# Hybrid encoder block on one core: the query product of the memory attention as seven block products, with weight sums kept in device memory and the key turn moved into the memory projection

## What is computed

```python
h = rms_norm(x, norm_xa_pre[l])
mn = rms_norm(mem, norm_mem[l])
q = (h @ xa_wq[l]).reshape(B, S, XA_HEADS, XA_HEAD_DIM)          # 1024x1024 by 1024x1024
kv = (mn @ xa_wkv[l]).reshape(B, M, 2, XA_HEADS, XA_HEAD_DIM)    # 256x1024 by 1024x2048
s = jnp.einsum('bshd,bmhd->bhsm', q, kv[:, :, 0]).astype(jnp.float32) * (XA_HEAD_DIM ** -0.5)
```

## Time and profile before

| | us |
|---|---|
| median of 3 runs | 1470.1 |
| range of the runs | 1470.03 to 1470.73 |
| profiled execution | 1470.84 |
| its span in the profile | 1468.9 |
| PE busy | 1431.9 |
| POOL busy | 785.4 |
| DVE busy | 681.4 |
| ACT busy | 588.4 |

### The profile page before, as it was taken

How to read it: one execution, slowest core, us unless ns; L and a number is a source line. 1 busy time by engine, 2 the same in 40 slices (tenths; PEclk the granted TensorE clock), 3 DMA queues, 4 the chain that set the end, 5 groups by cost and what they waited for, 6 DMA issues and landing times.

```text
span 1468.9 us, 20008 instructions
## 1 busy us (share of the span) xinstructions
PE 1431.9 (97%) x7192; PEld 1197.3 (82%) x7192; DVE 681.4 (46%) x1125; ACT 588.4 (40%) x1225; POOL 785.4 (53%) x607
## 2 busy tenths in 40 slices
PE   7999999998999999999999999999999999999998
PEld 7999999756988777877778888888888888767886
DVE  5181048586884760006136843333333323243868
ACT  6111112676633661125346533333333333434454
POOL 1454445001963365420235577777777775599753
PEclk9999999999999999999999999999999999999999
DMA  4311112000024143110124333333333224933364
GB/s 190 96 50 45 48 47 63 0 2 1 23 85 181 55 147 108 50 43 1 58 65 165 122 101 103 99 108 108 108 108 96 90 87 151 365 102 93 100 204 155
DMA packets 106292, 140.33 MB, mean 96 GB/s; under 512 B 8160, under 2 KB 61664, under 8 KB 106208
## 3 DMA queue, kind: packets, MB, share of 16 engines
q1 hardware_dynamic: 102480, 129.00, 27.0%
q10 hardware_dynamic: 3728, 10.24, 1.9%
HBM read 110.64 MB, written 28.57 MB: 95 GB/s over the span
## 4 chain that ended last, share of the span: by engine, by line
PE 84%; DVE 5%; POOL 3%; ACT 3%; DMA 2%; issue 2%; POOLq 0%; SPq 0%; DVEq 0%; ACTq 0%
PE ps L926 24%; PE ps L928 24%; PE ps L927 24%; PE ps L922 4%; PE ps L1273 2%; PE ps L1248 2%; DVE z L2331 1%; PE ps L1053 1%; PE ps L1147 1%; POOL w_lo L801 1%; POOL wd L895 1%; PE ps L1081 1%; DMA gain_b<-f_rows 1%; PE ps L1125 1%; DMA raw<-in_xa_wkv_dram 1%
## 5 line engine op out<-in xcount | busy, mean ns | idle before, releaser
L926 PE MATMUL ps<-w_hi,t_hi 128*128 128x352 f32 (+1 forms) x768 | 268.3, 349 | 3.0 <-DVE t_lo L2451 1.4
L928 PE MATMUL ps<-w_hi,t_lo 128*128 128x352 f32 (+1 forms) x768 | 266.5, 347 | 0.0
L927 PE MATMUL ps<-w_lo,t_hi 128*128 128x352 f32 (+1 forms) x768 | 266.1, 346 | 0.0
L726 POOL TENSOR_TENSOR w_hi<-raw,zero 128x352 fp32r<-128x352 f32 (+1 forms) x84 | 75.2, 895 | 174.5 <-PE ps L928 174.5
L926 PEld LDWEIGHTS ps<-w_hi,t_hi 128*128 128x128 f32 x768 | 145.2, 189 | 15.0 <-DVE t_lo L2451 2.2
L928 PEld LDWEIGHTS ps<-w_hi,t_lo 128*128 128x128 f32 x768 | 145.1, 189 | 10.8
L927 PEld LDWEIGHTS ps<-w_lo,t_hi 128*128 128x128 f32 x768 | 145.2, 189 | 10.4
L815 POOL TENSOR_TENSOR w_lo<-raw,w_hi 128x512 fp32r<-128x512 f32 x32 | 41.7, 1317 | 118.7 <-ACT w_hi L1774 118.7
L730 POOL TENSOR_TENSOR w_lo<-raw,w_hi 128x352 fp32r<-128x352 f32 (+1 forms) x84 | 95.8, 1140 | 6.6
L1542 ACT ACTIVATE z<-ps 128x352 f32 x48 | 22.4, 466 | 162.0 <-PE ps L928 161.5
L2564 DVE TENSOR_TENSOR ev<-ps,ev 128x512 f32<-128x512 f32 x21 | 14.5, 691 | 144.2 <-PE ps L928 144.2
...
## 6 DMA issues: line engine op xcount, KB each, us to landing
...
```

The lines of the kernel that those rows point to most:

```text
L726: nc.gpsimd.tensor_tensor(hi[:, s, 0:width], raw[:, s, 0:width], zero[:, 0:1].broadcast_to([P, width]), ALU.add).then_inc(w_rounded, 1)
L926: nc.tensor.matmul(out, a_hi, b_hi, start=start, stop=False, skip_group_check=onto)
L927: nc.tensor.matmul(out, a_hi, b_lo, start=False, stop=False, skip_group_check=onto)
L928: return nc.tensor.matmul(out, a_lo, b_hi, start=False, stop=stop, skip_group_check=onto)
```

## The change

The two operands are cut in 2x2 blocks: weights A (features of q by input features), tokens B (input features by halves of the tokens). Seven products of 512x512 blocks, in the order 11, 12, S1, S4, S2, S3, 22, take the place of eight; each is four units of four tiles, 12 matmuls a unit, 28 units. 11 and 12 use the weights and tokens as they are (of the first half of the tokens), S1 to S4 use sums of weight blocks, and S1, S4, S2, S3, 22 use or follow sums of token blocks.

- Weight sums: in the input projection SP loads the four blocks of `xa_wq` in four rounds into free columns of `z` (4 transfers of 256 KB a round), GpSimd makes four sums a round, one behind each split of units 12 to 27, SP stores them to `w_sums` in device memory.
- Token sums: the first (b12 - b11) is made on the rows, before they are turned, by a 512-wide subtraction in `pre_rows` for tiles 4 to 7. The others are made from the split parts: `tok_sum` (VectorE, three dependent operations of 128x1024), `tok_round` (ScalarE), `tok_low_part` (VectorE), six times.
- `tq_sum`, `tq_hi`, `tq_lo` lie where x1 was: SP stores x1's eight rows to device memory between the loads of the third memory product, and loads them back behind the query weights, ahead of the output weights.
- Query weights are rounded by ScalarE (`q_round`) and no longer by GpSimd, which keeps the low parts.
- After 11 and 12, ScalarE copies four banks each; after S1, S4, S2, S3 and 22 VectorE adds four banks each to `qX` (`q_join`).
- PE turns the keys between units 4 and 5 of the third memory product, into banks 4 to 7; ScalarE copies them behind its eighth rounding and ahead of the copies of that product. Tiles 4 and 5 are turned into these banks, each half once its bank's key copy is done.
- Loops of SP and GpSimd in the input projection are written out. The semaphores used are old ones at higher counts.

```diff
--- before.py
+++ after.py
@@ -56,14 +56,15 @@
-U_XO = U_Q + 2 * NK
+U_XO = U_Q + 7 * RING
...
-TILES = dict(z=0, oa=56, o=63, kv=77, q=81, xo=95, f=109)
+TILES = dict(z=0, oa=56, o=63, kv=77, q=81, xo=81)
+TURNED_K = TURNED["h2"] + 8
@@ -116,7 +117,17 @@
 def kv_seen(c, t):
-    return ACT_EV["h2"] + 6 * c + t + 1
+    return ACT_EV["h2"] + 6 * c + t + 1 + (4 if c >= 2 else 0)
+def h2_turned(t):
+    return TURNED["h2"] + 2 * t + (4 if t >= 4 else 0)
+PRODUCTS_Q = ("11", "12", "S1", "S4", "S2", "S3", "22")
+WEIGHT_SUMS = ("S1", "S2", "S3", "S4")
...
@@ -441,6 +462,32 @@
     return hi[:, k % RING, 0:ZW], lo[:, k % RING, 0:ZW]
+def sum_stage(r, b):
+    c = (ZP - 1) * ZW if r % 2 == 0 else (ZP - 2) * ZW
+    return z[:, 2 * b:2 * b + 2, c:c + 256]
+def two(ap):
+    return ap.rearrange("p (t f) -> p t f", t=2)
+def q_weights(n):
+    kind, k = PRODUCTS_Q[n // RING], n % RING
+    if kind in WEIGHT_SUMS:
+        return w_sums[WEIGHT_SUMS.index(kind), k]
+    i, j = int(kind[0]) - 1, int(kind[1]) - 1
+    return wq_v[RING * j + k, :, i * 512:(i + 1) * 512]
+def tok_sum_of(i, h):
+    lower, k = slice(0, 512), slice(2 * h, 2 * h + 2)
+    upper, kk = slice(512, 1024), slice(4 + 2 * h, 6 + 2 * h)
+    b11, b12 = (t_hi[:, k, lower], t_lo[:, k, lower]), (t_hi[:, k, upper], t_lo[:, k, upper])
+    b21, b22 = (t_hi[:, kk, lower], t_lo[:, kk, lower]), (t_hi[:, kk, upper], t_lo[:, kk, upper])
+    t2 = (tq_hi[:, k, :], tq_lo[:, k, :])
+    return ((t2, b22, b12), (b11, t2, b11), (b21, b21, t2))[i]
@@ -587,8 +634,31 @@
         sp.dma_start(z[:, t, 0:D], x_v[t]).then_inc(x_in[t], 16)
-    with sp.Fori(1, ZP) as c:
-        piece(c * NK + U_Z, win_v, bass.ds(c * ZW, ZW), ZW)
+    def sums_load(r):
+        if r >= 2:
+            sp.wait_ge(sums_out[r % 2], SUMS_OUT + 64 * (r // 2))
+        for b, (j, i) in enumerate(((0, 0), (1, 0), (0, 1), (1, 1))):
+            sp.dma_start(sum_stage(r, b), two(wq_v[RING * j + r % RING, :, i * 512:(i + 1) * 512])).then_inc(
+                sums_in[r % 2], 16)
+    def sums_store(r):
+        sp.wait_ge(summed_w, SUMMED_W + 4 * (r + 1))
+        for b, n in enumerate((1, 3, 0, 2)):
+            sp.dma_start(two(w_sums[n, r % RING]), sum_stage(r, b)).then_inc(sums_out[r % 2], 16)
+    for n in range(NK, ZP * NK):
+        c, k = divmod(n, NK)
+        load(c * NK + U_Z, k, raw[:, k % RING, 0:ZW], win_v[k, :, c * ZW:(c + 1) * ZW])
+        i = n // RING - 2
+        if n % RING == RING - 1:
+            if n == NK + RING - 1:
+                sp.wait_ge(w_split, NK)
+            if 2 <= i < SUM_ROUNDS + 2:
+                sums_store(i - 2)
+            if i < SUM_ROUNDS:
+                sums_load(i)
@@ -599,8 +669,18 @@
             load(U_KV + c * NK, k, dst, src)
-    with sp.Fori(0, 2) as c:
-        piece(c * NK + U_Q, wq_v, bass.ts(c, 512), 512)
+        if 2 * NK <= n < 3 * NK:
+            t = n - 2 * NK
+            sp.wait_ge(added, t + 1)
+            sp.dma_start(x1_rows[t], x1[:, t, :]).then_inc(x1_out, 16)
+    for i in range(2):
+        sp.wait_ge(sums_out[i], SUMS_OUT + 64 * SUM_ROUNDS // 2)
+    for n in range(7 * RING):
+        load(U_Q, n, raw[:, n % RING, :], q_weights(n))
+    sp.wait_ge(w_used, U_Q + 5 * RING)
+    sp.wait_ge(tok_low, TOK_LOW + 6)
+    for t in range(NT):
+        sp.dma_start(x1[:, t, :], x1_rows[t]).then_inc(x_in[t], 16)
@@ -737,11 +817,31 @@
         nc.gpsimd.tensor_tensor(lo, first_raw(k), hi.bitcast(F32), ALU.subtract).then_inc(w_split, 2 if k else 1)
+    def weight_sums(r, step):
+        a11, a12, a21, a22 = (sum_stage(r, b) for b in range(4))
+        done = SUMMED_W + 4 * r
+        if step == 0:
+            pool.wait_ge(sums_in[r % 2], SUMS_IN + 64 * (r // 2 + 1))
+            nc.gpsimd.tensor_tensor(a21, a21, a22, ALU.add).then_inc(summed_w, 1)
+        elif step == 1:
+            pool.wait_ge(summed_w, done + 1)
+            nc.gpsimd.tensor_tensor(a11, a21, a11, ALU.subtract).then_inc(summed_w, 1)
+        elif step == 2:
+            pool.wait_ge(summed_w, done + 2)
+            nc.gpsimd.tensor_tensor(a12, a12, a11, ALU.subtract).then_inc(summed_w, 1)
+        else:
+            nc.gpsimd.tensor_tensor(a22, a22, a11, ALU.subtract).then_inc(summed_w, 1)
...
+        else:
             split(c * NK + U_Z, U_Z, k, ZW, loads=c * 2)
+        r = n // RING - 3
+        if 0 <= r < SUM_ROUNDS:
+            weight_sums(r, n % RING)
@@ -804,9 +904,11 @@
             mem_low(n)
-    with pool.Fori(0, 2) as c:
-        for k in range(NK):
-            split(c * NK + U_Q, U_Q, k, 512, loads=c * 2)
+    for n in range(7 * RING):
+        k = n % RING
+        pool.wait_ge(q_rounded, Q_ROUNDED + n + 1)
+        nc.gpsimd.tensor_tensor(w_lo[:, k, :], raw[:, k, :], w_hi[:, k, :].bitcast(F32),
+                                ALU.subtract).then_inc(w_split, 1)
...
@@ -1195,11 +1299,26 @@
     def turn_tile(stage, n0, t):
+        def bank_free(half):
+            if t >= 2:
+                pe.wait_ge(dve_ev, DVE_EV[stage] + 2 * (t - 2) + half + 1)
+            if t in (4, 5):
+                pe.wait_ge(act_ev, kv_seen(1, 1) + 4 + 2 * (t - 4) + half + 1)
         turn_rows(t, lambda j: y[:, t, j * P:(j + 1) * P], 4 + 2 * (t % 2),
-                  lambda: pe.wait_ge(scaled, n0 + t + 1),
-                  lambda half: pe.wait_ge(dve_ev, DVE_EV[stage] + 2 * (t - 2) + half + 1) if t >= 2 else None)
+                  lambda: pe.wait_ge(scaled, n0 + t + 1), bank_free)
     pe.wait_ge(dve_ev, DVE_EV["h2"])
+    def turn_keys():
+        pe.wait_ge(act_ev, kv_seen(1, 1))
+        pe.wait_ge(dve_ev, DVE_EV["h2"] + 8)
+        for i in range(4):
+            for j in range(4):
+                kt, mt = divmod(4 * i + j, NM)
+                last = transpose_to(4 + i, j * P, kst[:, mt, kt * P:(kt + 1) * P])
+            last.then_inc(turned, 1)
@@ -1209,35 +1328,52 @@
         product(c * NK + U_KV, NM, 512, lambda t: pe.wait_ge(act_ev, kv_seen(c - 2, t)) if c >= 2 else None,
-                rows_by_weights(m_hi, m_lo, 512), b0=2 * (c % 2), ready=lambda k: kv_ready(c * NK + k))
+                rows_by_weights(m_hi, m_lo, 512), b0=2 * (c % 2), ready=lambda k: kv_ready(c * NK + k),
+                between=turn_keys if c == 2 else lambda: None)
...
         turn_tile("h2", NT + NM, 2 * c + 1)
...
+    def query_product(j):
+        kind = PRODUCTS_Q[j]
+        half, kk = {"11": (0, 0), "12": (0, 4), "S1": (512, 0), "S4": (512, 4), "S3": (0, 0), "22": (0, 4)}.get(kind, (0, 0))
+        high, low = (tq_hi, tq_lo) if kind == "S2" else (t_hi[:, kk:kk + 4, half:half + 512],
+                                                         t_lo[:, kk:kk + 4, half:half + 512])
+        first, b0 = kind in ("11", "S1", "S2"), 4 if kind in ("S1", "S4") else 0
+        for k in range(RING):
+            pe.wait_ge(w_split, U_Q + RING * j + k + 1)
+            if kind in ("S2", "S3", "22") and k % 2 == 0:
+                pe.wait_ge(tok_low, TOK_LOW + 2 * ("S2", "S3", "22").index(kind) + k // 2 + 1)
+            for m in range(4):
+                if k == 0:
+                    if kind == "11":
+                        pe.wait_ge(act_ev, kv_seen(2 + m // 2, m % 2))
+                    elif kind == "12":
+                        pe.wait_ge(q_copied, Q_COPIED + m + 1)
+                    elif kind == "S1" and m == 0:
+                        pe.wait_ge(dve_ev, DVE_EV["h3"])
+                    elif kind == "S4":
+                        pe.wait_ge(q_joined, Q_JOINED + m + 1)
+                    elif kind == "S2":
+                        pe.wait_ge(q_copied, Q_COPIED + 4 + m + 1)
+                    elif kind == "S3":
+                        pe.wait_ge(q_joined, Q_JOINED + 8 + m + 1)
+                    elif kind == "22":
+                        pe.wait_ge(q_joined, Q_JOINED + 12 + m + 1)
+                w = slice(m * P, (m + 1) * P)
+                last = three(ps[:, b0 + m, :], w_hi[:, k, w], w_lo[:, k, w], high[:, k, :], low[:, k, :],
+                             first and k == 0, k == RING - 1, not first)
+                if m == 3:
+                    last.then_inc(w_used, 1)
+                elif k == RING - 1:
+                    last.then_inc(q_done, 1)
+    for j in range(7):
+        query_product(j)
+    pe.wait_ge(q_joined, Q_JOINED + 20)
...
@@ -1733,7 +1863,21 @@
     round_units(RING)
+    def q_round(n):
+        act.wait_ge(w_loaded[n % RING], 16 * ((U_Q + n) // RING))
+        act.wait_ge(w_used, U_Q + n - RING + 1)
+        nc.scalar.activation(w_hi[:, n % RING, :], raw[:, n % RING, :], ACT.Copy).then_inc(q_rounded, 1)
     for c in range(4):
+        if c == 2:
+            for i in range(4):
+                act.wait_ge(turned, TURNED_K + i + 1)
+                nc.scalar.activation(kM[:, 2 * i:2 * i + 2, :], bank(4 + i).rearrange("p (k m) -> p k m", k=2),
+                                     ACT.Copy).then_inc(act_ev, 1)
+        if c == 3:
+            for n in range(3):
+                q_round(n)
@@ -1744,24 +1888,65 @@
```

(90 more changed lines are left out.)

70 lines of the change are left out of this document (35 added, 35 removed).

## The result

The changed kernel takes 1472.88 us (median of 20 runs, 1469.91 to 1476.27) beside 1471.3 us for the kernel before on the same chip (20 runs, 1469.73 to 1472.03). The ratio is 1.0014, 95% interval 1.0008 to 1.0021: slower by 1.6 to 2 us where 1.9 us less was forecast. The direction was wrong; the time is inside the range, close to its upper end.

What follows compares the result with a forecast made beforehand. PE, busy 97% of the span, was taken as the bound. Terms -11.2 + 1.1 + 2.4 + 5.7 + 0.1 = -1.9 us gave 1468.9 against the profiled 1470.84, 1468.2 against the median; range 1462.0 to 1473.0.

Steps and rivals of the forecast that it cites:

- The matmuls: Query product: 336 matmuls, 48 fewer, of the same shape at 0.2336 us each, -11.2 us.
- Weight sums: Input projection: GpSimd's 512-wide sums fit beside its splits within PE's 3.82 us per unit, so 0.
- Stall 1: Query product, unit 17: PE waits for weights rounded behind token sums, 0 to 2.8 us, taken as +2.4.
- Stall 2: Query product, unit 21: the last token sum's chain holds back the weight rounding, 5.1 to 6.0 us, taken as +5.7.
- The clock: Rival: TensorE drops to half rate in the second query stall, +2.6 to +3.8 us, 1470.8 to 1472.0; chance 0.18.
- The stores of x1: Third memory product: eight 512 KB stores between loads that run a few us ahead of need, taken as 0.
- part (d): Memory projection, fourth edit: SP issues eight stores between the third product's loads, 1.26 us each at best, taken as 0.
- rival 4: Stores choke the third memory product's loads and the ring gives way, +6 us net, 1474; chance 0.12.
- The other edits of the memory projection: Memory projection: row subtractions +0.8, moved key turns -1.2 and -1.7, late key copies +3.2, together +1.1 us.
- the key copies: Memory projection: ScalarE's four copies stand behind a late rounding, so turns of tiles 4 and 5 end later, +3.2 us.
- Reload of x1: Eight reloads queued ahead of the output weights' loads, 10.1 us, hidden behind the query product, so 0.
- Hand-over: End of the query product: a join of 0.69 us takes the place of a copy of 0.60, +0.1 us.

Runs made afterwards that it cites:

- e1: Changed kernel with ScalarE's order alone altered: weight roundings 16 to 19 and 20 to 24 put ahead of two token-sum roundings; 1463.51 us, ratio to before 0.9947.
- e2: Changed kernel with only weight roundings 21 to 24 put ahead of the last token-sum rounding; 1465.34 us, ratio to before 0.9963.
- e3: Changed kernel with 18 extra matmuls of 128x512, whose result nobody reads, in PE's wait ahead of query unit 21; 1470.61 us, ratio to before 1.0001.
- e4: Changed kernel with key turn and key copies moved from the third memory product to behind the first query product; 1471.17 us, ratio to before 1.0.
- e9: Changed kernel with x1's stores earlier: rows 0 to 5 behind the fourth memory weight load, 6 and 7 behind the last; 1469.94 us, ratio 0.9997.
- e8: Kernel before with only eight 512 KB stores of x1 added between the loads of the third memory product; 1474.13 us, ratio 1.0022.
- e10: Changed kernel with e1's order of roundings and e9's early stores together; 1460.42 us, ratio to before 0.9927, one run of 3668.92 us left out of the ratio.

## Why the prediction was wrong, step by step

- **The matmuls, -11.2: right.** 48 fewer, spacing 0.2336, shown bare in e1 (78.25 us against the forecast 78.5).
- **Weight sums at 0: right.** The last matmul ahead of the memory projection starts at 500.51, before at 500.83. The sums of 512 columns take 1.32 to 1.56 us on average in POOL's rows, inside the 1.24 to 1.9 that the prediction allowed.
- **Stall 1, +2.4: 2.2 in the profile, 1.8 by e2 against e1. Stall 2, +5.7: 5.3.** Both at their places, units 17 and 21, by the chain that was written down. The prediction's own chain for stall 1 gives 16.6 - 14.0 = 2.6 us as the upper end, not the 2.8 that it states. In the second one VectorE's three sums took 3.7 us and met GpSimd nowhere, since GpSimd waited for the same roundings. The upper ends, to which the rule of the Trainium skill led ("SBUF — State Buffer", "Who interferes with whom"), were not reached.
- **The clock, taken as a rival with 0.18: it came.** This is the first step that failed. The prediction had the chain of stall 2, its length of over 5 us and the slow start of the program, priced the fall at 2.6 to 3.8 us, and yet kept it out of the sum, which assumed full speed behind both stalls. The profile has 14 matmuls at 0.43 us and a granted clock of 0.52 behind the stall, 2.8 us, and e3 shows that filling the stall takes them away. By the page "TensorE: Matmul & The Clock Gate" of the Trainium skill, "What's actually happening", idling brings the half rate; the trace agrees. The same stall of 5.50 us in e4 and e9 cost 1.7 and 1.8 us of clock, so 2.8 is the largest price seen. What the rival did not have is the second fall, behind the 2.5 us wait for the keys, another 1.3 us in the profiled execution.
- **The stores of x1, taken as 0:** 1.8 to 2.4 us in the profiles of the changed kernel, 2.9 us in its median (e9), 3.3 us in the kernel before (e8). This is the second step that failed, part (d) of the memory projection. "The loads run a few us ahead of need" was not read from a row: ACT's roundings already waited 15.2 us for loads from 500 to 565 us before, and wait 19.0 after. The mechanism of rival 4 was right in the main, at a third to a half of its price of 6 us: a load's landing went from 3.3 to 5.2 us and the ring passed it on, with no wait of PE for a load by name; it shows in waits for low parts and keys, while the DMA engines' busy share from 524 to 536 us rose from 0.51 to 0.97.
- **The other edits of the memory projection, +1.1: 0.0** (e10, 60.41 against 60.38). Its terms were off: the key copies hold PE for 2.2 to 2.5 us ahead of tile 4 (forecast 3.2), and the row subtractions take 1.65 us and not 0.7. GpSimd is busy in all four of them, the case that the prediction itself read from 1.22 against 2.20 us. Moving them away gave 0.4.
- **Reload of x1 at 0: right.** SP issues it at 633.60, the output weights are rounded from 649.23 on, and the first exponential waits for VectorE:

```profile
633.60 5.34 SPq L683 DMA_DIRECT2D x<-x_rows  x8
```

```profile
659.30 0.47 ACT L1969 ACTIVATE px<-ps,wnm 128x256 f32<-128x256 f32 x1 [3.98 <-DVE wnm L2688]
```

- **Hand-over, +0.1:** 1.18 against 1.17 us.

In the profiled execution -1.9 became +2.6. The difference of 4.5 us is the clock, 2.8 + 1.3 = 4.1, and the memory projection without its fall, 62.5 - 60.4 - 1.1 = 1.0, less 0.6 for the two stalls. In the medians the difference is 3.5 us: the profiled execution of the kernel before lies 0.5 us under its median of 1471.3, that of the changed kernel 0.5 above. The clock's share holds beyond the one profile. The mean granted clock averages 0.9962 over the 20 runs of the changed kernel and 0.9989 to 0.9990 over those of the kernel before beside the experiments, which is 4 us over 1470 (an estimate). The times follow it: the seven runs of the changed kernel at 0.993 to 0.995 took 1473.74 to 1476.27 us, the seven at 0.998 took 1469.91 to 1473.01.

So the matmuls and the stalls came as the sum had them, and what turned the sign are two things that it put at nothing: the clock and the stores.

Two things stay open. How often the clock falls behind the wait for the keys was not counted: a run's mean does not tell the two falls apart, and a profile shows one execution. And why the late stores are worth 2.9 us in the medians but 1.8 to 2.4 in the profiles is not shown; it is not the clock, whose mean is the same with early stores.
